# Two accumulators of gathered tokens folded into one before TensorE sums them

## What is computed

```python
def peer_ffn(xn, w_q, sub_keys, u, v):
    ...
    best_s, pos = lax.top_k(cand_s, PEER_TOPK)
    ids = jnp.take_along_axis(cand_i, pos, axis=-1).reshape(T, PEER_HEADS * PEER_TOPK)
    gates = jax.nn.softmax(best_s, axis=-1).reshape(T, PEER_HEADS * PEER_TOPK)
    ...
    def chunk(args):
        x_c, ids_c, g_c = args
        act = jax.nn.gelu(jnp.einsum('td,ted->te', x_c, u[ids_c]), approximate=False)
        return jnp.einsum('te,ted->td', g_c.astype(x_c.dtype) * act, v[ids_c])
```

## Time and profile before

| what | value |
|---|---|
| median of 3 runs | 975.21 us (974.95 to 975.78) |
| the profiled execution's own time | 973.53 us |
| its span | 971.6 us |
| busy: TensorE, VectorE, ScalarE, GpSimd | 961.6, 790.6, 550.5, 486.8 us |
| mean granted clock of TensorE | 0.998 |

### The profile page before, as it was taken

How to read it: one execution, slowest core, us unless ns; L and a number is a source line. 1 busy time by engine, 2 the same in 40 slices (tenths; PEclk the granted TensorE clock), 3 DMA queues, 4 the chain that set the end, 5 groups by cost and what they waited for, 6 DMA issues and landing times.

```text
span 971.6 us, 18460 instructions
## 1 busy us (share of the span) xinstructions
PE 961.6 (99%) x7031; PEld 931.1 (96%) x7031; DVE 790.6 (81%) x1546; ACT 550.5 (57%) x979; POOL 486.8 (50%) x315
## 2 busy tenths in 40 slices
PE   8999999999999999999999999999999999999997
PEld 8999899999999999999998888889999999999997
DVE  5858666455999999999988787777899899999896
ACT  7786556546555646464555575555555555555556
POOL 1000001001388888888888888827388873313310
PEclk9999999999999999999999999999999999999999
DMA  9689764624638787778778877879999999999991
GB/s 317 216 301 339 247 226 157 204 88 138 210 60 202 171 213 182 208 177 198 208 189 209 195 177 187 205 208 309 330 360 351 327 361 367 351 352 371 372 331 65
DMA packets 134107, 235.12 MB, mean 242 GB/s; under 512 B 38592, under 2 KB 87488, under 8 KB 133664
## 3 DMA queue, kind: packets, MB, share of 16 engines
q1 hardware_dynamic: 97392, 208.14, 64.2%
q0 software_dynamic: 36224, 25.70, 13.9%
q10 hardware_dynamic: 432, 0.57, 0.2%
HBM read 216.38 MB, written 17.97 MB: 241 GB/s over the span
## 4 chain that ended last, share of the span: by engine, by line
PE 97%; ACT 1%; DVE 1%; DMA 0%; issue 0%; ACTq 0%; DVEq 0%
PE acc L1399 23%; PE acc L1655 11%; PE bank L1655 11%; PE bank L1620 9%; PE bank L1589 8%; PE bank L1588 8%; PE bank L1590 8%; PE bank L1656 5%; PE acc L1656 5%; PE bank L1621 5%; PE bank L1573 1%; PE bank L1497 1%; PE bank L1364 1%; PE bank L1519 1%; PE bank L1428 0%; DMA xr<-x 0%
## 5 line engine op out<-in xcount | busy, mean ns | idle before, releaser
L468 POOL DMA_INDIRECT wmap<-gate,widx x192 | 319.1, 1662 | 90.3 <-issue 59.2
L750 ACT ACTIVATE hl<-raw 128x1024 fp32r<-128x1024 f32 x192 | 202.9, 1058 | 84.4 <-DMA raw<-v 30.4
L1120 DVE TENSOR_TENSOR hl<-raw,hl 128x1024 fp32r<-128x1024 f32 x99 | 121.0, 1223 | 25.2 <-ACT hl L750 22.8
L491 POOL DMA_INDIRECT vg<-v,idx_v x48 | 76.9, 1602 | 118.1 <-DVE acc_s L1261 97.8
L1588 PE MATMUL bank<-xt,hl 128*128 128x256 f32 x480 | 135.9, 283 | 0.0
L1589 PE MATMUL bank<-xt,hl 128*128 128x256 f32 x480 | 135.8, 283 | 0.0
L1590 PE MATMUL bank<-xt,hl 128*128 128x256 f32 x480 | 135.7, 283 | 0.0
L1127 DVE TENSOR_TENSOR hl<-raw,hl 128x512 fp32r<-128x512 f32 x186 | 119.4, 688 | 17.0 <-ACT hl L750 14.2
L1655 PE MATMUL acc<-whl,hl 128*128 128x416 f32 x380 | 121.4, 370 | 0.0
L1655 PE MATMUL bank<-whl,hl 128*128 128x416 f32 x380 | 120.9, 368 | 0.0
L1399 PE MATMUL acc<-xt,wsp 128*128 128x256 f32 x960 | 119.1, 284 | 0.1
(11 more groups left out here) (292 smaller groups left out, 2253.8 us busy)
## 6 DMA issues: line engine op xcount, KB each, us to landing
raw<-u_t SPq DMA_DIRECT2D x128, 512.0 KB
raw<-v SPq DMA_DIRECT2D x128, 512.0 KB
wmap<-zeros SPq DMA_DIRECT2D x6, 2048.0 KB, 11.8
wblk<-wmap SPq DMA_DIRECT2D x62, 192.0 KB
wraw<-w_in SPq DMA_DIRECT2D x9, 1024.0 KB, 9.4
wraw<-w_pq SPq DMA_DIRECT2D x8, 1024.0 KB, 5.2
wraw<-w_ck SPq DMA_DIRECT2D x4, 1024.0 KB, 7.9
wraw<-w_cv SPq DMA_DIRECT2D x4, 1024.0 KB, 7.5
```

Source lines behind the costliest of these rows:

```text
L468: nc.gpsimd.indirect_dma_start(out=wmap, out_offset=bass.IndirectOffsetOnAxis(ap=set_ranks(widx, k)[:, h, r:r + 1], axis=0), in_=set_ranks ...
L750: nc.scalar.activation(eslot(k, 0, second), raw[:, k // 2, k % 2], ACT.Copy).then_inc(ready, 1)
L1120: V.tensor_tensor(eslot(k, 1, second), raw[:, k // 2, k % 2], eslot(k, 0, second).bitcast(F32), ALU.subtract).then_inc(ready, 1)
```

## The change

Once all 48 gathered steps are done, SP issues two transfers inside SBUF: the upper 64 partitions of the first accumulator go to the lower 64 of a new tile `shifted`, and the lower 64 of the second go to its upper 64. VectorE then adds twice, so that `acc_s[:, 0]` holds the 32 tokens of the first set in partitions 0 to 63 and the 16 of the second in 64 to 127. One selector of 48 columns, with zeros where the sets don't meet, serves both. TensorE waits for the two adds (`s_fold`), and has one matmul of 48 columns a chunk in place of one of 32 and one of 16.

```diff
@@ -103,6 +103,7 @@
         act_w = at("act_w", 24 * K, [KEYS, DT])
         vg = at("vg", 0, [NVG, D])
         acc_s = at("acc_s", 12 * K, [2, D])
+        shifted = at("shifted", 20 * K, [D])
         fin = at("fin", 24 * K, [DC, T])
         ysq = at("ysq", 32 * K, [DC, T])
         orow = at("orow", 40 * K, [TT, D])
@@ -226,6 +227,7 @@
         s_wh1, s_wl1 = sem("s_w1_first_high"), sem("s_w1_first_low")
         s_rtr, s_xe, s_xa = sem("s_residual_transposed"), sem("s_residual_taken"), sem("s_residual_added")
         s_run, s_ft, s_fina, s_fgd = sem("s_squares_run"), sem("s_fin_turned"), sem("s_fin_act"), sem("s_fin_gain_dve")
+        s_fold, s_shift = sem("s_sparse_folded"), sem("s_sparse_shifted")
         s_us = sem("s_u_halves_added")
         s_stg, s_sst, s_sbk, s_ix = (sem(n) for n in (
             "s_sparse_staged", "s_sparse_stored", "s_sparse_back", "s_sparse_index"))
@@ -405,6 +407,9 @@
                     sp.dma_start(flat(xr2[:]), xres).then_inc(s_xr2, 16)
                 if j % 2 and (j + 3) // 2 < NWB:
                     weights((j + 3) // 2)
+            sp.wait_ge(s_fma, NSD)
+            sp.dma_start(shifted[0:64], acc_s[64:P, 0]).then_inc(s_shift, 16)
+            sp.dma_start(shifted[64:P], acc_s[0:64, 1]).then_inc(s_shift, 16)
             for k in range(2):
                 sp.wait_ge(s_fin, k + 1)
                 q = slice(512 * k, 512 * k + 512)
@@ -949,8 +954,9 @@
             V.tensor_copy(tcol[:, 2:3], posu[:, 1, 0:1])
             link(V.tensor_copy(tcol[:, 4:5], posu[:, 1, 1:2]))
             V.tensor_scalar(tcol[:, 5:6], tcol[:, 4:5], float(NSA), None, ALU.add)
-            V.tensor_scalar(sel[:, 0:NSA], iota[:, 0:NSA], tcol[:, 2:3], None, ALU.is_equal)
-            V.tensor_scalar(sel[:, NSA:NS], iota[:, 0:NSB], tcol[:, 4:5], None, ALU.is_equal)
+            link(V.memset(sel[:], 0.0))
+            V.tensor_scalar(sel[0:64, 0:NSA], iota[0:64, 0:NSA], tcol[0:64, 2:3], None, ALU.is_equal)
+            V.tensor_scalar(sel[64:P, NSA:NS], iota[64:P, 0:NSB], tcol[64:P, 4:5], None, ALU.is_equal)
 
             dve.wait_ge(s_spc, 1)
             e, z, z2, q, sp8 = c4(1), c4(2), c4(3), c4(4), c4(5)
@@ -1325,6 +1331,9 @@
                 dve.wait_ge(s_ysp, c + 1)
                 V.tensor_tensor(fin[:, c], fin[:, c], xr2[:, c], ALU.add).then_inc(s_xa, 1)
 
+            dve.wait_ge(s_shift, 32)
+            V.tensor_tensor(acc_s[0:64, 0], acc_s[0:64, 0], shifted[0:64], ALU.add).then_inc(s_fold, 1)
+            V.tensor_tensor(acc_s[64:P, 0], acc_s[64:P, 1], shifted[64:P], ALU.add).then_inc(s_fold, 1)
             for c in range(DC - 1):
                 residual_add(c)
             for c in range(DC):
@@ -1674,9 +1683,7 @@
                 return last
 
             def sparse_sum(c):
-                for k, q in enumerate((slice(0, NSA), slice(NSA, NS))):
-                    pe.matmul(vbank(c)[:, DT + q.start:DT + q.stop], acc_s[:, k, P * c:P * c + P], sel[:, q], start=False,
-                              stop=False, skip_group_check=True)
+                pe.matmul(vbank(c)[:, DT:T], acc_s[:, 0, P * c:P * c + P], sel[:], start=False, stop=False, skip_group_check=True)
 
             for j in range(8):
                 pe.wait_ge(s_vl, j + 1)
@@ -1690,7 +1697,7 @@
             for j in range(KEYS - 8, KEYS - 2):
                 ahead = None
                 if j == KEYS - 3:
-                    pe.wait_ge(s_fma, NSD)
+                    pe.wait_ge(s_fold, 2)
                     ahead = sparse_sum
                 pe.wait_ge(s_vl, j + 1)
                 pe.wait_ge(s_Wl, j // 2 + 1)
```

## The result

| | before | changed |
|---|---|---|
| time, median (lowest to highest, runs) | 975.48 us (974.95 to 976.07, 6) | 983.88 us (982.52 to 985.90, 6) |
| ratio, 95% interval | 1 | 1.0093 [1.0082, 1.0104] |
| profiled execution: time, span | 973.53, 971.6 us | 984.82, 982.9 us |
| mean granted clock of TensorE | 0.998 | 0.992 |

The medians differ by 8.4 us, and the ratio gives 9.1 (0.0093 x 975.5), where 5.0 were predicted. The sign and the place were right; the median lies 1.4 us above the range of 977.9 to 982.5.

What follows compares the result with a forecast made beforehand. The prediction took TensorE to bound the kernel. Stall 5.15, minus saving 1.8, plus slow clock 1.6 gave +4.95 us on a median of 975.21, so 980.2 us, with a range of 977.9 to 982.5.

Steps and rivals of the forecast that it cites:

- What bounds the kernel: TensorE, busy 961.6 of 971.6 us; a stall ahead of key 125 moves the whole finish.
- The saving, 1.8 us: Key 125's eight chunks on TensorE: two sum passes each instead of four, 1.8 us saved, 0.9 at the lower end.
- The stall, 5.15 us (4.55 to 5.75): TensorE ahead of key 125 waits for the fold and starts at 957.25 instead of 952.09.
- step 2, "they land": The two SBUF transfers of the fold land at 954.7, the middle between 954.1 and 955.3.
- a rival of 10%: Transfers between partition halves are slow and land 1.4 us later than assumed: 981.6 us; chance 10%.
- The room ahead of TensorE's arrival: The last gathered accumulate was done 0.47 us before TensorE came to key 125.
- The clock, 1.6 us (0 to 3.2): TensorE's clock halves in the stall, staying slow for 3.4 us of work in the finish; 1.6 us lost.
- the rival: The slow clock in the finish lasts twice as long and costs 3.2 us: +6.6, 981.8 us; chance 15%.
- The edits costed at nothing: Memset of `sel` and its wait, perhaps 0.3 us on VectorE but covered by idling; adds stand ahead of residual adds without cost.
- The sum: Whole kernel: 5.15 - 1.8 + 1.6 = +4.95 us, so 980.2 us as the median.
- The high end of the sum, 982.4: Whole kernel, longest stall and dearest clock together: 975.21 + 5.75 - 1.8 + 3.2 = 982.4 us.
- Not slower: the fold is ready in time.: No stall at key 125 because the fold is done in time; the saving alone is left, 973.4 us; chance 5%.

Runs made afterwards that it cites:

- Experiment 10: Changed kernel with the dense matmuls of keys 125 and 126 ahead of the wait, the eight sums behind it, then key 127: 976.57 us.
- experiment 1: Kernel before with one 48-column matmul a chunk on the first accumulator, old wait, no moves or adds, second accumulator left out: 973.27 us.
- experiment 5: Changed kernel with the same bytes moved in two transfers over all 128 partitions, sums not those wanted: 982.82 us, one run.
- experiment 4: Kernel before with the change's tile and two semaphores declared but not used: 974.68 us, ratio 0.9997 to the kernel before.
- experiment 11: Changed kernel with the fold in two parts, first half moved in SP's key 100, second in key 126, steps ending after key 118: 974.19 us.
- experiment 6: Changed kernel with the same wait, but behind it key 125's 16 dense matmuls first and the eight sums after them: 984.31 us.
- experiment 9: Changed kernel with key 125's dense matmuls run two extra times ahead of the wait, output not the reference's: 978.96 us, in two groups.
- experiment 7: Changed kernel with the last gathered step after key 116, moves in SP's key 125, adds after VectorE's keys 120 and 121: 975.13 us.
- experiment 2: Changed kernel with moves, adds and wait, but adds to a spare tile and both accumulators summed as before: 987.72 us.
- experiment 3: Changed kernel with 64 matmuls of 48 columns ahead of the wait, output not the one wanted: 988.59 us.
- experiment 8: Changed kernel with the last gathered step after key 111, moves in SP's key 120, adds after VectorE's keys 120 and 121: 974.53 us.

## Why the prediction was right in kind and too small

- **What bounds the kernel.** Right. Every us of stall at key 125 reached the end: with the other items it makes up the 11.3 us between the spans. Experiment 10 shows that this is the order's doing: with two keys ahead, the same chain costs 2 us.
- **The saving, 1.8 us.** Right (experiment 1).
- **The stall, 5.15 us (4.55 to 5.75).** Mis-sized: 6.4. The chain was right link by link: issue 0.02 us after the accumulate, two transfers, two adds of 1.22 with the second 1.25 after the first. What failed is step 2, "they land", taken at 954.7 or 3.1 us after the accumulate's end (951.62): they landed at 957.8, 4.3 after it (953.50). That such a transfer "may be slower" stood in the prediction as a remark, and as a rival of 10% that put the landing 1.4 us later; it is what happened, 1.3 later. Full-width moves made a fold of 5.6 us (experiment 5, one run), the 5.5 of the prediction. The room ahead of TensorE's arrival, the number on which the change was said to turn, isn't fixed either: 0.47 us before, 0.44 after, but 1.9 in experiment 4 and 3.1 in experiment 10.
- **The clock, 1.6 us (0 to 3.2).** This is the step that failed most: 4.8 us. That it falls was right. Its length was carried over from the program's start (3.4 us of work), and the rival doubled it to 6.8; in the changed kernel it was 10.4 us of work. The start gave only one sample of one mix, and one read from the length of the weight loads alone: the granted clock of that stretch stands at 1.00 in the trace of before.

```profile
2.20:5.58 3.38, 3.37 (x16) 3.37 (x17) 0.00 (x0) 1.52 (x4) 1.85 (x11) 1.00 0.86 325
```

- **How long it stays down.** The slow clock lasted 3.4 us in dense keys (experiment 11), 5.1 where key 125's dense matmuls came first (experiment 6, one execution), 6.8, 10.2 and 12.9 in experiments 9, 7 and 5, and some 14 in experiment 2 with twice the sums. That the small sums among the dense matmuls keep the clock down is what this pattern suggests, with experiment 3 beside it. It is argued, not shown: experiment 6's other runs didn't get faster, and behind its wait the same order of key 125 gave anything from 6.8 to 12.9. What sets the length is open.
- **What a short stall does.** Not in the prediction at all, which took the fall 1.55 us into the idle time at the very end as its measure. In the changed kernel it came 3.1 us into the stall, in experiments 5 and 6 some 4.1 and 4.6. Stalls of 1.93 and 2.53 us ended with the clock at 1.00, and it fell 1.7 and 1.5 us into the work. In experiments 7 and 9 the runs lie in two groups, 6 to 7 us apart, and the mean clocks say that the fall is what parts them.
- **The edits costed at nothing.** The profile shows no cost of them: the selector's memset and compares take 0.4 us more, and VectorE then idles 2.47 us for ScalarE's split in place of 2.87; the adds delay no residual add beyond what TensorE's own delay does.
- **The sum.** +9.4 in the profile without the upstream wait, +9.1 by the ratio, +8.4 in the medians; predicted +4.95. Of the 4.4 missing in the profile, 1.3 are the landing and 3.2 the clock. The high end of the sum, 982.4, joined both high ends and was still 1.5 us short, because both were too low: 5.75 for a stall of 6.4, 3.2 for a clock loss of 4.8.
- **"Not slower: the fold is ready in time."** Its condition was right, and experiments 7, 8 and 11 aimed at it by moving the steps. Experiment 7 met it only in part: its profile has a stall of 2.53 us. None of them paid the 1.8 us that the rival gave it. Moves among the loads of `v` land after 5 to 8 us, and the profiles show waits for split rows, one of which pulled the clock down. Some of these waits stand ahead of every move, so not the moves but the closer steps or chance must be behind them; these two weren't separated, and where the 1.8 us went isn't shown in full.

## What to carry to other kernels

Before you shorten work on the bounding engine by adding a chain in front of it, measure how much room the chain's first link has, and count the whole chain: here two passes a chunk were worth 1.8 us and the fold behind them took 6.8. Price a stall of TensorE as the stall plus a stretch of half-speed work behind it, and don't take that stretch from another mix of matmuls; with waits of about 2 us, some executions took over 6 us more than others of the same kernel. If the chain must be there, put full-sized work ahead of the wait in the engine's own order.

## What the runs showed of the hardware

- The granted clock can fall after the idle time is over: 1.5 us after work resumed behind 2.53 us of idling, 1.7 behind 1.93, 1.1 behind 1.85. A gap and the slow stretch behind it don't stand at the same place in a trace.
- Matmuls of 48 columns, back to back for 10.6 us, did not hold the clock at 1.00, though the profile calls TensorE fully busy.
- Transfers inside SBUF from SP land 2.3 us after the issue at full width (256 KB each, two of them), 3.1 and 3.7 us between partition halves; among the loads of `v`, 5 to 8 us.
